# A two-layer hybrid decoder step: reordered TensorE work in prompt tiles and at the end of a layer

## The reference, cut to what matters

```python
z = rmsnorm(x, g_pre) @ w_in                  # one projection, split into the inputs below
(cq, ckv, kpe, gate_mla, gq, gk, gv, gg, gate_gla, mq, gate_mem) = split(z)
q = rope(rmsnorm(rmsnorm(cq) @ w_uq))         # 8 heads x 96, from a 384-wide query latent
c = rmsnorm(ckv)                              # 256-wide key/value latent
k = rope(rmsnorm([c @ w_uk, kpe]))            # keys of the heads; values are c @ w_uv
mla = softmax(q k^T, causal) @ (c @ w_uv)
gla = gated_linear_attention(gq, gk, gv, gg)  # a running state, in chunks
mem = softmax(rmsnorm(mq) mk^T) @ mv          # mk, mv: 256 memory rows, per layer
x = x + concat(silu(gate_mla)*mla, silu(gate_gla)*rmsnorm(gla), silu(gate_mem)*mem) @ w_out
```

## Time and profile before

| what | value |
|---|---|
| median of 3 runs | 3052.71 us (3043.8 to 3052.93) |
| the profiled execution | 3058.52 us, its span 3056.7 us |
| PE busy | 2976.0 us, 97% of the span |
| DVE busy | 1589.0 us, 52% |
| ACT busy | 1038.6 us, 34% |
| mean granted TensorE clock | 0.986 |

### The profile page before, as it was taken

How to read it: one execution, slowest core, us unless ns; L and a number is a source line. 1 busy time by engine, 2 the same in 40 slices (tenths; PEclk the granted TensorE clock), 3 DMA queues, 4 the chain that set the end, 5 groups by cost and what they waited for, 6 DMA issues and landing times. The chain is left out here.

```text
span 3056.7 us, 56023 instructions
## 1 busy us (share of the span) xinstructions
PE 2976.0 (97%) x20297; PEld 1824.5 (60%) x20297; DVE 1589.0 (52%) x3551; ACT 1038.6 (34%) x2159; POOL 328.0 (11%) x465
## 2 busy tenths in 40 slices
PE   7999999999999999999999999999899999999999
PEld 4666666655555565555456667666455555655554
DVE  3665655545665545554145565556456555455531
ACT  1333333323434434442023333334134444344410
POOL 1110000001111101110000001000111111111100
PEclk9999999999999999999999999999999999999999
DMA  7000000013122212223520000000411222122222
GB/s 269 27 17 17 17 17 17 14 54 106 48 55 59 58 44 59 59 79 111 192 92 17 16 19 26 13 9 14 127 48 49 60 55 61 44 56 61 95 91 79
DMA packets 192166, 179.57 MB, mean 59 GB/s; under 512 B 93769, under 2 KB 171666, under 8 KB 189842
## 3 DMA queue, kind: packets, MB, share of 16 engines
q1 hardware_dynamic: 190144, 175.18, 18.6%
q10 hardware_dynamic: 1746, 0.81, 0.1%
HBM read 153.41 MB, written 22.50 MB: 58 GB/s over the span
## 5 line engine op out<-in xcount | busy, mean ns | idle before, releaser
L1303 DVE TENSOR_REDUCE w_in<-w_in 128x8 f32<-128x512 f32 x512 | 351.2, 686 | 577.7 <-ACT w_in L805 574.3
L1802 PE MATMUL ps<-w_uk,region 128*128 128x512 f32 x1248 | 588.2, 599 | 1.3
L1415 PE MATMUL ps<-w_in,xT 128*128 128x256 f32 (+9 forms) x1952 | 547.6, 434 | 2.9 <-DVE xT L924 2.9
L1415 PEld LDWEIGHTS ps<-w_in,xT 128*128 128x128 f32 (+1 forms) x1952 | 353.6, 185 | 157.1 <-issue 73.7
L1802 PE MATMUL ps<-w_uk,xT 128*128 128x512 f32 x800 | 383.6, 607 | 0.9 <-ACT w_in L805 0.3
L805 ACT ACTIVATE w_in<-ps 128x512 f32<-128x512 f32 x512 | 305.8, 597 | 217.2 <-PE ps L1802 201.2
L1802 PEld LDWEIGHTS ps<-w_uk,region 128*128 128x128 f32 x1248 | 216.6, 191 | 191.9 <-issue 191.1
L536 POOL TENSOR_TENSOR rs<-us,mhalf 128x1 f32<-128x1 f32 (+4 forms) x132 | 130.9, 991 | 1413.4 <-DVE us L964 759.0
L1802 PEld LDWEIGHTS ps<-w_uk,xT 128*128 128x128 f32 x800 | 141.8, 195 | 128.0 <-issue 128.0
L784 ACT COPY region<-ps 128x512 f32<-128x512 f32 x156 | 91.5, 586 | 279.4 <-PE ps L1789 278.1
L1789 PEld LDWEIGHTS ps<-ident,region 128*128 128x128 f32 x960 | 116.8, 142 | 109.3 <-issue 109.2
(11 more groups left out here) (389 smaller groups left out, 3928.8 us busy)
## 6 DMA issues: line engine op xcount, KB each, us to landing
region<-in_cache_ckv SPq DMA_DIRECT2D x480, 128.0 KB, 2.0
w_in<-in_w_in SPq DMA_DIRECT2D x16, 1240.0 KB, 11.3
mix_rows<-xn SPq DMA_DIRECT2D x16, 512.0 KB, 2.9
region<-in_cache_kpe SPq DMA_DIRECT2D x512, 16.0 KB, 1.8
region<-in_w_out SPq DMA_DIRECT2D x8, 1024.0 KB
xt<-in_x_prompt SPq DMA_DIRECT2D x11, 512.0 KB, 4.1
xt<-x_mid SPq DMA_DIRECT2D x11, 512.0 KB, 4.9
region<-in_w_mem_kv SPq DMA_DIRECT2D x2, 2048.0 KB, 23.9
```

The lines of the kernel that those rows point to most:

```text
L1303: tell(dve.tensor_reduce(pst[:, 0, j * H:j * H + H], heads(sqb[:, j % 2, :], H), X, ALU.add), s.pkn_red, np_)
L1415: ins = mm(out, xT[:, k, 0:T], w_in[:, k, c0:c0 + w], start=k == 0, stop=k == KD - 1)
L1802: ins = mm(ps[:, 2 + j % 2, :], page[:, o_:o_ + P], w_uk[:, c, :], start=c == 0, stop=c == 1)
```

## The change

Seven edits in the written order; no arithmetic is added or left out.

1. In prompt tiles n > 0 the first of eight chunks of the query latents moves ahead of the wait for the turned memory queries; seven stay where they were.
2. In all prompt tiles the values are made right behind the queries, without the wait for the keys' evacuation. ACT evacuates them first, and the turned keys now wait for that copy, since both use PSUM bank 1.
3. Two of eight chunks of the memory gate move from ahead of the turned queries to behind them.
4. In tile 0 the second block of memory keys is made later on DVE and POOL, and turned later on PE and DVE.
5. The layer's turned first rows: PE turns them ahead of the sample tile's output, DVE copies them ahead of the sample tile's addition.
6. `m_T` is swapped: turned rows of even tiles, the sample tile's among them, lie in `glw`, those of odd tiles in `xT`.
7. The sample tile's output waits for one half of the last prompt tile's addition instead of both.

```diff
-        m_T = (xT, glw)
+        m_T = (glw, xT)
...
# POOL, tile 0: the roots of the second layer's memory keys
+                        if n == 0 and i in (M_CQ, M_K):
+                            l = (M_CQ, M_K).index(i)
+                            rsqrt(mem_mean(1, l), 9 + 8 * l, MH, P)
...
# ACT
                         act.wait_ge(s.kqv_ps, 3 * (TP * L + t) + 1)
+                        tell(act.copy(vv[:, t, :], ps[:, 1, :]), s.v_evac, TP * L + t)
+                        act.wait_ge(s.kqv_ps, 3 * (TP * L + t) + 2)
                         tell(act.copy(kT[...], ...), s.kT_evac, TP * L + t)
-                        act.wait_ge(s.kqv_ps, 3 * (TP * L + t) + 2)
+                        act.wait_ge(s.kqv_ps, 3 * (TP * L + t) + 3)
                         tell(act.copy(qT, ...), s.qT_evac, TP * L + t)
-                        act.wait_ge(s.kqv_ps, 3 * (TP * L + t) + 3)
-                        tell(act.copy(vv[:, t, :], ps[:, 1, :]), s.v_evac, TP * L + t)
...
# DVE, tile 0
                         mem_heads(1, 0)
-                        mem_heads(1, 1)
...
-                    if n == 0:
-                        turned_mem_keys(1)
                     dve.wait_ge(s.ssq_ready, n + 1)
...
                     tell(ts(cq[0:T, :], ...), s.cq_ready, n)
+                    if n == 0:
+                        mem_heads(1, 1)
...
                         tell(cp(ptT[:, :, :], ...), s.mpT_evac, m)
+                    if n == 0:
+                        turned_mem_keys(1)
...
# DVE, output stage (and the same two calls gone from the start of the layer)
+                    if t == TP and L + 1 < DEPTH:
+                        turned_x(0, 0, L + 1)
+                        turned_x(0, 1, L + 1)
                     added(t, 1 if t < TP else 0)
...
# PE
                     if pm_:
+                        if n:
+                            project_part(ps[0:T, 3, 0:QR], T, O_CQ, QR, 0, 1)
                         pe.wait_ge(s.mqT_evac, n + 1)
...
-                        project(ps[0:T, 3, 0:QR], T, O_CQ, QR).then_inc(s.cq_ps, 1)
+                        project_part(ps[0:T, 3, 0:QR], T, O_CQ, QR, 1, KD).then_inc(s.cq_ps, 1)
...
                     if pm_:
+                        if n == 0:
+                            pe.wait_ge(s.mkT_evac, 2)
+                        for c in range(2):
+                            ins = mm(ps[:, 1, :], cT[:, c, :], w_uv[:, c, :], start=c == 0, stop=c == 1)
+                        ins.then_inc(s.kqv_ps, 1)
                         pe.wait_ge(s.mpT_evac, m + 1)
                         project(ps[0:T, 7, 0:GW], T, O_GGLA, GW)
...
                         pe.wait_ge(s.k_ready, n + 1)
+                        pe.wait_ge(s.v_evac, m + 1)
...
-                        project(ps[0:T, 7, GW:GW + MW], T, O_GMEM, MW).then_inc(s.gates_ps, 1)
+                        project_part(ps[0:T, 7, GW:GW + MW], T, O_GMEM, MW, 0, KD - 2)
                         pe.wait_ge(s.q_ready, n + 1)
...
-                        pe.wait_ge(s.kT_evac, m + 1)
-                        for c in range(2):
-                            ins = mm(ps[:, 1, :], cT[:, c, :], w_uv[:, c, :], start=c == 0, stop=c == 1)
-                        ins.then_inc(s.kqv_ps, 1)
+                        project_part(ps[0:T, 7, GW:GW + MW], T, O_GMEM, MW, KD - 2, KD).then_inc(s.gates_ps, 1)
...
# PE, output stage
+                if L + 1 < DEPTH:
+                    turn_x(0, 0, L + 1)
+                    turn_x(0, 1, L + 1)
                 n, p = NT * L + TP, TP % 2
                 pe.wait_ge(s.mT_evac, n + 1)
                 pe.wait_ge(s.mT_evac_a, n + 1)
-                pe.wait_ge(s.y_ready, n_y(L, TP))
+                pe.wait_ge(s.y_ready, n_y(L, TP) - 1)
```

More of the change, by code:

```diff
@@ L282, in mem_mean @@
         def mem_mean(L, t):
-            return 3 + 5 * L + t
+            return (3, 4, 8, 10)[2 * L + t]
         def order_of(t):
@@ L291, in mean @@
             i = order_of(t).index(i)
-            return 7 + 7 * n + i if n else 5 + i + (2 if i > 2 else 0)
+            return 7 + 7 * n + i if n else 5 + i + (1 if i > 2 else 0) + (1 if i > 3 else 0)
         def mean_of_x(n):
@@ L549, in _ @@
                             continue
+                        if n == 0 and i in (M_CQ, M_K):
+                            l = (M_CQ, M_K).index(i)
+                            rsqrt(mem_mean(1, l), 9 + 8 * l, MH, P)
                         if i == M_X:
                             rsqrt(mean_of_x(n + 1), 0, 1, tok(t + 1))
-                            if n == 0:
-                                for l in range(2):
-                                    rsqrt(mem_mean(1, l), 9 + 8 * l, MH, P)
                         else:
@@ L919, in norm_x, with turned_x @@
                     tell(ts(x_[0:T, :], x_[0:T, :], rs[0:T, 0:1], None, ALU.mult), s.xn_ready, n)
-                def turned_x(t, i):
+                def turned_x(t, i, L=L):
                     n, T, w = NT * L + t, tok(t), slice(4 * i, 4 * i + 4)
@@ L947, in _ @@
                     dve.wait_ge(s.rows_in, 16 * (7 + 6 * L))
-                    turned_x(0, 0)
-                    turned_x(0, 1)
                 for t in range(NT):
@@ L1414, in project, with project_part @@
                 for k in range(KD):
+                    ins = mm(out, xT[:, k, 0:T], w_in[:, k, c0:c0 + w], start=k == 0, stop=k == KD - 1)
+                return ins
+            def project_part(out, T, c0, w, k0, k1):
+                for k in range(k0, k1):
                     ins = mm(out, xT[:, k, 0:T], w_in[:, k, c0:c0 + w], start=k == 0, stop=k == KD - 1)
@@ L1468, in _, with turn_x @@
             for L in range(DEPTH):
-                def turn_x(t, i):
+                def turn_x(t, i, L=L):
                     n, T = NT * L + t, tok(t)
@@ L1486, in project_mq @@
                     project(ps[0:T, 6, 0:MW], T, O_MQ, MW).then_inc(s.gvmq_ps, 1)
-                turn_x(0, 0)
-                turn_x(0, 1)
                 if L == 0:
+                    turn_x(0, 0)
+                    turn_x(0, 1)
                     pe.wait_ge(s.w_in_in, 16)
@@ L1572, in _ @@
                     if n == 0:
-                        turn_mem_keys(1)
-                        pe.wait_ge(s.mk_ready, 4)
+                        pe.wait_ge(s.mk_ready, 3)
                     pe.wait_ge(s.cT_evac, n + 1)
@@ L1583, in _ @@
                         ins.then_inc(s.mpT_ps, 1)
+                    if n == 0:
+                        turn_mem_keys(1)
                     pe.wait_ge(s.cq_ready, n + 1)
@@ L1636, in _ @@
                         project(ps[0:T, 3, :], T, O_GMLA, H * VD).then_inc(s.gates_ps, 1)
-                        pe.wait_ge(s.v_evac, m + 1)
                         for h in range(H):
```

## The result

The changed kernel's median is 3035.3 us (6 runs, 3033.94 to 3038.63). The kernel before, run beside it, had 3052.82 us (6 runs, 3043.8 to 3054.35). The ratio is 0.9949, with a 95% interval of 0.9934 to 0.9964: it is faster. The two medians lie 17.5 us apart; the ratio, taken over the runs, is 15.6 us (0.0051 of 3052.8), with an interval from 11.0 to 20.1 us (0.0036 and 0.0066). The forecast was a gain of 10.9 us, just under that interval, and 3041.8 us: inside the stated range, 6.5 us above the median.

A forecast was written before the change was run, and what follows sets the result against it. PE, busy 97% of the span, bounds the kernel, so only its stalls can give time. The terms 0 + 4.6 + 1.4 + 3.9 + 0.95 = 10.9 us take the median of 3052.7 to 3041.8 us, range 3032 to 3049.

The forecast's parts named there:

- a sum of 10.9: Whole kernel: gains of 0 + 4.6 + 1.4 + 3.9 + 0.95 us, from 7 to 14 us by the bounds.
- The signs: Changed profile: GLA scores wait about 0.6 us, turned queries nearly none, first scores 0.3 to 0.5; layer 1's projection without DVE wait.
- rival B: Turned queries: PE comes late by the 0.3 us it would win, so the order there pays nothing; 3046.4 us, chance 22%.
- The 0.05 us between L1021 and L1560: GLA scores, tiles n > 0: PE starts 0.05 us after DVE's instruction ends, so the stall only moves; gain nothing.
- 0.29 us a tile: First scores, 16 prompt tiles: begin 0.40 us earlier, less 0.11 for the first pass after a wait; 4.6 us in all.
- the 0.11 us taken from the earlier trace: First scores: cost of the first pass after a wait, from 1.00 us after a wait against 0.89 with its load fetched ahead.
- a whole load of 0.19 us: First scores: by the skill's rule alone, nothing is in flight when ACT is done; edits 2 and 3 would give 3.4 us.
- The bounds (0 to 2.2): Tile 0: nothing if turning the keys holds the query latents; 2.2 us if the half clock of this stretch goes too.
- 4.2 (the upper bound): Layer boundary: 3.9 us from two waits removed, taken as 2.9 to 4.2 us depending on when the last `w_in` load lands.
- the same step leads to 3041.8 us: Whole kernel: the 10.9 us gain taken off 3052.7 us, the median of the runs shown; chance 63%.
- Rival A: Memory and GLA scores: DVE reaches L1021 earlier too, so edit 1 gives 8.9 us on top; 3032.9 us, chance 10%.
- Rival C: New stalls at GLA scores and first scores bring 1.2 GHz stretches, 1.7 us in each of 15 tiles; 3067.3 us, chance 5%.

The follow-up runs named there:

- second profiles of either kernel: Profiles from running both kernels again unchanged: the kernel before, median 3049.75 us (ratio 1.0003), and the changed kernel, median 3037.69 us (ratio 0.9946).
- its repeat: The kernel before, run once more with nothing changed: median 3049.75 us over 12 runs, ratio 1.0003.
- The padded kernels: Changed kernel with unused 128x512 products ahead of layer 1's projection: with 12, median 3046.7 us (ratio 0.999); with 6, 3038.29 us (0.9961).
- the copy in halves: Changed kernel with ACT's copy of the turned queries in two halves: median 3036.53 us; with edit 4 undone as well, 3034.35 us.

## Why the prediction was right, and where it was short

**The mechanism held, term by term.** The comparison that leaves most of the clock out is between the second profiles of either kernel: their sample stretches agree within 0.1 us and their page groups within 0.02. The spans differ by 3042.9 - 3032.3 = 10.6 us, against a sum of 10.9. Some clock is left in it: 1.7 us for the changed kernel at the boundary, and about 1.0 us against it in each layer, in the tiles behind the low stretches at its start. The lowest runs of all differ by 3043.73 - 3033.94 = 9.8 us. Runs of the same mean granted clock say the same: at 0.992 the changed kernel took 3033.9 and 3034.1 us, and 27 runs of before have a median of 3044.7; at 0.990 four runs lie at 3037.4 to 3039.4, and 16 of before have a median of 3049.6. That is 10.7 and 11.3 us. The signs came as named: 0.54 us of wait at the GLA scores, the turned queries 0.06 us after the rotation's end (rival B needed 0.2), the first scores 2.30 us after it, and layer 1's projection at the end of the sample output.

- Edit 1: forecast 0, measured 0.00 to 0.02 us a tile. The 0.05 us between L1021 and L1560 said it.
- Edits 2 and 3: forecast 0.29 us a tile, measured 0.28 to 0.32. The first pass after the new wait costs 0.10 us (0.91 against 0.81 us), near the 0.11 us taken from the earlier trace rows. The prediction's estimate from the Trainium skill (TensorE: Matmul & The Clock Gate, Step-by-step: what each phase is for), where weight loads are pulled ahead of matmuls in flight, had the scores lose a whole load of 0.19 us; they lost 0.10.
- Edit 4: forecast 1.4 us, measured 1.28 where tile 0 kept its clock, -1.2 for the whole of tile 0 in the first profile. The bounds (0 to 2.2) left out that the low stretch could move onto the queries.
- Edits 5 to 7: forecast 3.9 and 0.95 us, measured 4.2 (the upper bound) and 1.0. `w_in` was in when the projection came.

The upper bound of edit 4 had a second fault. In the kernel before, the low stretch of tile 0 cost nothing, since PE still waited 0.72 us for DVE at the turned queries:

```profile
95.69 1.08 PE L1614 MATMUL ps<-ident,ws 128*96 128x128 f32 x8 [0.72 <-DVE ws L868]
```

In the second profile of the changed kernel the low stretch was gone, and the gain was still 1.28 us.

**The step that fell short is the last one of the sum**, "the same step leads to 3041.8 us": the gain was put on the median of the runs before as if both kernels had the same clock on average. The median gave 17.5 us. The first profiles show where it sat: 11.4 us in the sample tiles and in page group 17, stretches without an edit, of which a long and a short size turned up in the same program. The prediction named the spread of 3043.8 to 3052.9 us and added a few microseconds to the range for it, but no term to the sum.

The runs of before show how large this is. In all they number 89 with the twelve of its repeat, and they bunch: 30 lie below 3047 us (median 3044.7), 16 around 3049.7, 25 around 3054.5 and 18 around 3059.6. The 12 runs of the changed kernel lie at 3033.9 to 3036.0 (7) and 3037.4 to 3041.2 (5). Three runs were a thin base for a median that jumps in steps of 5 us. But more runs of before would not have closed the gap: the median of all 89 is 3050.6 us, which gives a forecast of 3039.7, and that of the 12 runs of the changed kernel is 3035.7. The other 4 us go with the clock: the median of the mean clocks is 0.991 for these 12 runs and 0.990 for the 83 of before that have one on record. The sum has no term for that.

**Rival A** fell with edit 1 alone. **Rival C** was right that the granted clock weighs as much as the edits, and wrong in place and sign: tiles 1 to 7 kept their gain of 0.3 us each behind the new stalls of 0.5 and 0.3 us, and the 11.4 us of long and short draws sit in stretches without an edit. Where the edits shortened long stalls, in tile 0 and at the layer boundary, low stretches became rarer, not more frequent. The sentence from the Trainium skill (TensorE: Matmul & The Clock Gate, Part 1: The HAM clock gate) that the low clock is the default and activity releases it does not by itself tell these draws: in page group 17 the profile shows PE busy for all 35.00 us of the stretch, and the clock was 0.80 in one execution and 0.90 in another. What busy means there is in the last section.

**What stays open** is why the long draws are rarer in the new order. Of ten layers in the profiles with the old order around the queries or with parts of the change on it, five had a sample stretch of 146.5 us or more; of fourteen in the profiles with edits 2, 3 and 5 to 7 together, one had. Counted from 145 us on, it is seven of ten against six of fourteen, so the profiles alone say little. The low stretch at the boundary, 1.7 us, was seen in two of four profiles with the old boundary and in none of the eight with the new one, and that is the only named piece of it. The padded kernels speak against the distance of the layers as the reason.

That the draws are the same for every order is unlikely, by the mean clock of the runs: of 83 runs of before 27 had 0.992; of the twelve with edits 2 and 3 alone none had more than 0.990, and of the eleven with the copy in halves none had more than 0.989. Which instructions decide it, no run here shows.

## What to carry to other kernels

A stall that is filled pays only if the next wait on that engine is not already binding: look for the gap between the next instruction and what it waits for, and where it is 0.05 us, cost the edit at nothing. Where a single program's times spread by 17 us, judge an edit of 5 to 10 us by the starts of the same instructions in two traces, piece by piece, and compare pieces without an edit first: what moves there is not the instructions that were moved. Comparing runs of the same mean granted clock is a second way. A forecast for such a kernel needs the distribution of its runs, not the median of three, and the change can shift that distribution too.

## What the runs showed of the hardware

The granted clock also falls in a stretch where the profile shows no idle time of PE. In page group 17 PE does 64 rows of 16 columns (start, us, instruction), in the first profile of before and then in its repeat:

```profile
1113.48 11.24 PE L1769 MATMUL ps<-w_in 128*128 128x16 f32 x64
1124.56 3.76 PE L1802 MATMUL ps<-w_uk,xT 128*128 128x512 f32 x4
...
1128.97 2.30 PE L1802 MATMUL ps<-w_uk,xT 128*128 128x512 f32 x4
```

```profile
1109.66 8.65 PE L1769 MATMUL ps<-w_in 128*128 128x16 f32 x64
1118.14 3.76 PE L1802 MATMUL ps<-w_uk,xT 128*128 128x512 f32 x4
...
1122.29 1.88 PE L1802 MATMUL ps<-w_uk,xT 128*128 128x512 f32 x4
```

The narrow products took 11.24 us in one execution and 8.65 in the other, at the lower of the two levels (1.2 GHz) for more or less of the time, and the wide products behind them caught the rest. In every profile here page group 17 of both layers has such a stretch. Busy does not mean that PE multiplies all the time there: the weight loads (second figure, PEld) fill the whole stretch of narrow products, here in the first profile at a mean clock of 0.62:

```profile
1113.48:1124.56 11.08, 11.08 (x66) 11.08 (x65) 2.42 (x7) 0.65 (x2) 0.00 (x0) 0.62 0.18 48
```

That narrow products bring the clock down is what the place suggests; no run changed their width, so it was not tested.
